# Query tiles and the last forget-head tiles as 512-column products in a two-layer fp32 trunk kernel

## The reference

```
h = h + 0.5 * swiglu(rms_norm(h, ffn1_norm), gate, up, down)       # 1024 -> 2816 -> 1024
h = h + token_mixing(rms_norm(h, mix_norm), w_in, ..., w_out)
h = h + 0.5 * swiglu(rms_norm(h, ffn2_norm), gate, up, down)
```

## Time and profile before

| what | us |
|---|---|
| median of 3 runs | 1005.8 (1005.06 to 1005.88) |
| the profiled execution | 1005.14 |
| its span, first to last instruction | 1003.3 |
| PE busy | 992.9 (99%) |
| PEld busy | 844.2 |
| DVE busy | 755.8 |
| ACT busy | 540.0 |
| POOL busy | 134.2 |

### The profile page before, as it was taken

The page is one execution under the profiler, slowest core; times in us unless marked ns, Lnnn a source line. Parts: engine busy times, 40 slices in busy tenths (PEclk is TensorE's granted clock), DMA queues, the critical chain, the costliest instruction groups (busy, mean ns, idle before and its releaser), DMA issues.

```text
span 1003.3 us, 16520 instructions
## 1 busy us (share of the span) xinstructions
PE 992.9 (99%) x5650; PEld 844.2 (84%) x5650; DVE 755.8 (75%) x1504; ACT 540.0 (54%) x978; POOL 134.2 (13%) x152
## 2 busy tenths in 40 slices
PE   9999999999999999999999999999999999999997
PEld 8888888888878888888888888889887788888885
DVE  6887777678667887777788777777786688777775
ACT  5555555566565555555555555555755555555553
POOL 1000000018761000000000000000197500000001
PEclk9999999999999999999999999999999999999999
DMA  8665555765534665555536555554563446555541
GB/s 297 205 205 188 187 187 188 251 225 173 208 106 151 218 196 188 188 188 188 189 128 212 191 187 189 187 187 148 185 210 131 167 150 223 191 188 188 188 146 42
DMA packets 38165, 184.76 MB, mean 184 GB/s; under 512 B 3904, under 2 KB 8176, under 8 KB 23920
## 3 DMA queue, kind: packets, MB, share of 16 engines
q1 hardware_dynamic: 33408, 178.60, 53.6%
q10 hardware_dynamic: 4720, 5.67, 1.8%
HBM read 183.18 MB, written 2.64 MB: 185 GB/s over the span
## 4 chain that ended last, share of the span: by engine, by line
PE 98%; DVE 1%; DMA 0%; ACT 0%; POOL 0%; issue 0%; DVEq 0%
PE ps L627 33%; PE ps L628 17%; PE ps L621 13%; PE ps L623 12%; PE ps L622 12%; PE ps L707 1%; PE ps L637 1%; PE ps L872 1%; PE ps L641 1%; PE ps L638 1%; PE ps L884 1%; PE ps L863 1%; PE ps L859 1%; DMA cst<-consts 0%; DVE wlo L1092 0%; PE ps L717 0%
## 5 line engine op out<-in xcount | busy, mean ns | idle before, releaser
L627 PE MATMUL ps<-xboth,whi 128*128 128x512 f32 x1440 | 508.0, 395 | 0.0
L628 PE MATMUL ps<-xboth,wlo 128*128 128x256 f32 x1440 | 403.4, 280 | 0.0
L627 PEld LDWEIGHTS ps<-xboth,whi 128*128 128x128 f32 x1440 | 269.9, 187 | 63.9 <-issue 1.0
L628 PEld LDWEIGHTS ps<-xboth,wlo 128*128 128x128 f32 x1440 | 272.0, 189 | 3.6
L1092 DVE TENSOR_TENSOR wlo<-raw,whi 128x1024 fp32r<-128x1024 f32 (+2 forms) x215 | 251.4, 1206 | 6.0 <-ACT whi L366 5.3
L366 ACT CAST whi<-raw 128x1024 fp32r<-128x1024 f32 (+1 forms) x222 | 217.5, 1029 | 7.4 <-PE ps L623 7.4
L1098 DVE TENSOR_TENSOR wlo<-raw,whi 128x1024 fp32r<-128x1024 f32 (+1 forms) x110 | 132.8, 1208 | 101.6 <-ACT whi L370 101.5
L408 ACT ACTIVATE sig<-hg 128x256 f32<-128x256 f32 x88 | 36.9, 420 | 199.0 <-DVE hg L1171 182.4
L370 ACT CAST whi<-raw 128x1024 fp32r<-128x1024 f32 (+1 forms) x112 | 112.8, 1007 | 53.4 <-PE ps L623 53.0
L623 PE MATMUL ps<-whi,hlo 128*128 128x512 f32 x352 | 138.9, 395 | 0.0
L622 PE MATMUL ps<-wlo,hhi 128*128 128x512 f32 x352 | 138.8, 394 | 0.0
(11 more groups left out here) (174 smaller groups left out, 1185.4 us busy)
## 6 DMA issues: line engine op xcount, KB each, us to landing
raw<-stream SPq DMA_DIRECT2D x111, 1024.0 KB, 5.2
raw<-stream SPq DMA_DIRECT2D x113, 512.0 KB, 3.6
decay<-table ACTq DMA_DIRECT2D x2, 1024.0 KB, 8.8
table<-table ACTq DMA_DIRECT2D x1, 1524.0 KB
X<-x SPq DMA_DIRECT2D x2, 512.0 KB, 5.4
bias<-table ACTq DMA_DIRECT2D x1, 1024.0 KB, 5.5
out<-feat SPq DMA_DIRECT2D x3, 256.0 KB, 2.4
cst<-consts SPq DMA_DIRECT2D x1, 576.0 KB, 11.2
```

Of the source, the lines that this page charges most:

```text
L627: nc.tensor.matmul(ps[:, bank, :], a[0], xboth[:, k, :], start=k == 0, stop=False)
L628: return nc.tensor.matmul(ps[:, bank, 0:S], a[1], xhi[:, k, :], start=False, stop=k == KT - 1)
```

## The change

All tiles of token mixing that were made by `three` are made by `wide`, in the same order on PE.

- The four index-query tiles: ACT's `query_out` copies the bank's second half to `tlo` instead of the whole result to `feat` (new semaphore `qlo_out`), at the same places of ACT's list. A new `query_sum` on DVE adds the first half and writes `feat`, and now it is what raises `qi_out`. Its four calls are put into DVE's list: after az, after logf (ahead of cn), and around the first half of `front(3)`.
- The last four forget tiles become `wide_tile(8)` to `wide_tile(11)` in the same two banks: ACT gets `tile_low(8)` to `tile_low(11)`, where it had only waited; DVE gets `tile_sum(8)` to `tile_sum(11)` in place of `tile_out`; POOL gets four more `scale`, between its `share` calls, and its two additions to `decay` come two heads later.

```diff
-NWIDE = 8
+NWIDE = 12
...
-                scale(l, 4, NWIDE)
+                scale(l, 4, 8)
                 for hh in range(2 * NH):
                     share(l, hh)
-                    if hh == 1:
+                    if hh in (0, 1, 3, 4):
+                        t = 8 + (0, 1, 3, 4).index(hh)
+                        scale(l, t, t + 1)
+                    if hh == 3:
                         pool.wait_ge(decay_in, (l + 1) * 16)
                         pool.wait_ge(const_in, 16)
-                    if hh in (1, 3):
+                    if hh in (3, 5):
...
                     act.wait_ge(feat_mm, l * NFEAT + j + 1)
-                    nc.scalar.copy(feat[:, j, :], ps[:, GU + j % 2, 0:S]).then_inc(qi_out, 1)
+                    nc.scalar.copy(tlo[j % 4], ps[:, GU + j % 2, S:2 * S]).then_inc(qlo_out, 1)
...
                     if p == 0:
-                        act.wait_ge(feat_mm, l * NFEAT + (FX + 5))
+                        tile_low(8)
                         front(7)
-                        act.wait_ge(feat_mm, l * NFEAT + (FX + 6))
+                        tile_low(9)
                         back(7)
                     if p == 1:
-                        act.wait_ge(feat_mm, l * NFEAT + NFEAT)
+                        tile_low(10)
+                        tile_low(11)
...
-                        t = three(ps[:, bank + j % 2, 0:S], w(s, at + k * P, P), xt(k), k == 0, k == KT - 1)
+                        t = wide(GU + j % 2, w(s, at + k * P, P), k)
...
-                    if g and h2 < 2:
+                    if g:
                         pe.wait_ge(scaled_out, l * NWIDE + (6 + 2 * h2))
-                    elif g:
-                        pe.wait_ge(feat_out, l * NTILE + (2 * h2 - 1))
...
-                tile(FX + 4, front(5), UNIT, bank=FILLB)
-                tile(FX + 5, back(5), FRONT, bank=FILLB)
+                wide_tile(8, front(5), UNIT)
+                wide_tile(9, back(5), FRONT)
...
+                def query_sum(j):
+
+                    dve.wait_ge(qlo_out, l * NQI + j)
+                    nc.vector.tensor_tensor(feat[:, j, :], ps[:, GU + j % 2, 0:S], tlo[j % 4], ALU.add).then_inc(qi_out, 1)
...
                                                op1=ALU.max).then_inc(az_out, 1)
+                query_sum(QI)
                 dve.wait_ge(css_mm, l + 1)
...
                 nc.vector.tensor_tensor(logf[:], mz[:], lz[:], ALU.subtract).then_inc(logf_out, 1)
+                query_sum(QI + 1)
                 dve.wait_ge(crows_mm, l + 1)
                 nc.vector.tensor_tensor(cn, ct, ps[:, CB, 0:S], ALU.mult).then_inc(cn_out, 1)
...
-                front(3)
+                query_sum(QI + 2)
+                front(3, (0,))
+                query_sum(QI + 3)
+                front(3, (1,))
...
                     if p == 0:
-                        tile_out(FX + 4, FILLB)
+                        tile_sum(8)
                         front(7)
-                        tile_out(FX + 5, FILLB)
+                        tile_sum(9)
                     if p == 1:
                         back(7)
-                        tile_out(FX + 6, FILLB)
                         turned(0)
-                        tile_out(FX + 7, FILLB)
+                        tile_sum(10)
                         turned(1)
+                        tile_sum(11)
```

More of the change, by code:

```diff
@@ L66 @@
 NQI = KA - QI
-NWIDE = 8
-NTILE = 1 + NFEAT - QA - NWIDE
+NWIDE = 12
 G_FFN1, G_MIX, G_FFN2, G_CKV, G_BF = 0, KT, 2 * KT, 3 * KT, 3 * KT + 1
@@ L183, in trunk, with tile_bank @@
         NPAIR = NH
-        TILEB = 5, 4, 3, 2
+        def tile_bank(t):
+            return (5, 4, 3, 2)[t % 4] if t < 8 else (3, 2)[t % 2]
         tlo = [t[:, i, :] for t in (ur, ht) for i in range(2)]
@@ L206, in trunk @@
         feat_mm, feat_out, ka_out, qi_out, wo_mm = sems("feat_mm feat_out ka_out qi_out wo_mm")
-        tlo_out, tsum_out, scaled_out = sems("tlo_out tsum_out scaled_out")
+        qlo_out, tlo_out, tsum_out, scaled_out = sems("qlo_out tlo_out tsum_out scaled_out")
         part_out, xg_out, fin_act = sems("part_out")[0], sems("xg_out0 xg_out1"), sems("fin_act")[0]
@@ L342, in _ @@
                 split_front(l, 5, 1)
-                scale(l, 4, NWIDE)
+                scale(l, 4, 8)
                 for hh in range(2 * NH):
                     share(l, hh)
-                    if hh == 1:
+                    if hh in (0, 1, 3, 4):
+                        t = 8 + (0, 1, 3, 4).index(hh)
+                        scale(l, t, t + 1)
+                    if hh == 3:
                         pool.wait_ge(decay_in, (l + 1) * 16)
                         pool.wait_ge(const_in, 16)
-                    if hh in (1, 3):
-                        nc.gpsimd.tensor_tensor(decay[:, :, (hh - 1) * P:hh * P], decay[:, :, hh // 2 * P + P:hh // 2 * P + S],
+                    if hh in (3, 5):
+                        at = (hh - 3) // 2
+                        nc.gpsimd.tensor_tensor(decay[:, :, 2 * at * P:(2 * at + 1) * P], decay[:, :, (at + 1) * P:(at + 2) * P],
                                                 cmask[:, P:S].unsqueeze(1).to_broadcast([P, NH, P]), ALU.add
@@ L512, in tile_low @@
                     act.wait_ge(feat_mm, l * NFEAT + (QA + t + 1))
-                    nc.scalar.copy(tlo[t % 4], ps[:, TILEB[t % 4], S:2 * S]).then_inc(tlo_out, 1)
+                    nc.scalar.copy(tlo[t % 4], ps[:, tile_bank(t), S:2 * S]).then_inc(tlo_out, 1)
                 relu_head(0)
@@ L566, in mix @@
                         act.wait_ge(vf_mm, l * 2 * 4 + 2 * 4)
+                        act.wait_ge(scaled_out, (l + 1) * NWIDE)
                         for b in range(NB):
@@ L796, in back, with tile @@
                     return m % 2
-                def tile(j, s, at, midway=None, bank=GU):
-                    if QI + 2 <= j < QA:
+                def tile(j, s, at, midway=None):
+                    if j >= QI + 2:
                         pe.wait_ge(qi_out, l * NQI + (j - 2))
[L804 to L807, removed]
                     for k in range(KT):
@@ L821, in wide_tile @@
                     else:
-                        pe.wait_ge(tsum_out, l * NWIDE + (t - 3))
+                        pe.wait_ge(tsum_out, l * NWIDE + (t - 3 if t < 8 else t - 1))
                     for k in range(KT):
-                        u = wide(TILEB[t % 4], w(s, at + k * P, P), k)
+                        u = wide(tile_bank(t), w(s, at + k * P, P), k)
                     u.then_inc(feat_mm, 1)
@@ L938, in index @@
                                          start=True, stop=True).then_inc(idx_mm, 1)
-                pe.wait_ge(feat_out, l * NTILE + 1)
+                pe.wait_ge(feat_out, l + 1)
                 pe.wait_ge(cn_out, l + 1)
@@ L983, in mix @@
                 logits(0)
-                tile(FX + 4, front(5), UNIT, bank=FILLB)
-                tile(FX + 5, back(5), FRONT, bank=FILLB)
+                wide_tile(8, front(5), UNIT)
+                wide_tile(9, back(5), FRONT)
                 logits(1)
-                tile(FX + 6, front(6, 0), 0, bank=FILLB)
+                wide_tile(10, front(6, 0), 0)
                 turn(0)
-                tile(FX + 7, front(6), UNIT, bank=FILLB)
+                wide_tile(11, front(6), UNIT)
                 turn(1)
@@ L1266, in tile_sum @@
                     dve.wait_ge(tlo_out, l * NWIDE + (t + 1))
-                    nc.vector.tensor_tensor(tsum[t % 4], ps[:, TILEB[t % 4], 0:S], tlo[t % 4], ALU.add
+                    nc.vector.tensor_tensor(tsum[t % 4], ps[:, tile_bank(t), 0:S], tlo[t % 4], ALU.add
                                             ).then_inc(tsum_out, 1)
```

## The result

The changed kernel is slower: median 1012.44 us (1009.31 to 1014.58, 4 executions) against 1005.84 (1005.06 to 1006.24), a ratio of 1.0066 with the 95% interval 1.0052 to 1.0079. The forecast was 1009.2 with a range up to 1012.4: the way was right, the size was not, and the median lies just outside the range.

What follows compares the result with a forecast made beforehand. PE was taken as the bound nearly everywhere, DVE's chain from cn before QI+3. DVE's wait +4.5 and shorter tiles -1.1 made +3.4 us, 1008.5 for the profiled execution, 1009.2 us for the median; range 1008.2 to 1012.4.

Steps and rivals of the forecast that it cites:

- The bound and the place: PE bounds nearly everywhere, but before QI+3 in each layer DVE's chain from cn does, with no slack behind cn.
- The costly step: QI+1's addition ahead of cn on DVE waits for ACT's copy behind three casts: 2.25 us a layer, +4.5 us.
- The tiles: QI+3 and four fill tiles behind PE's wait, each 0.11 us shorter as wide tiles: -1.1 us for both layers.
- QI's, QI+2's and QI+3's additions: DVE's other query additions, after az and around front(3): margins or idle time absorb them, cost nothing.
- the fill tiles: Last four forget tiles' new work on ACT, DVE and POOL: cost nothing, at most 0.3 us a layer.
- POOL's queue: Scalings added between POOL's shares: margins of 4.6 and 5.0 us before the transposes, cost nothing.
- One margin: Second head's transposes on PE after DVE's copy of the first head's: margin shrinks from 0.8 to 0.35 us.
- PE's clock falls in the longer stop: Rival, chance 0.27: PE's 2.9 us stop before QI+3 lowers its clock; 1010.8 us with one fall, 1012.4 with two.
- the likeliest case: The forecast itself, chance 0.60: longer waits before QI+3 but no clock fall, median 1009.2 us.
- The price of a fall: PE at the lower clock for as long as the 19 products at the start: 1.6 us each fall.
- The stop isn't there: Rival, chance 0.03: ACT copies QI+1 before its casts, so only the tiles' gain is left, 1004.1 us.
- The stalling fill stage: Rival, chance 0.07: PE waits at turn(1) or turn(2), 0.5 to 1 us a layer, 1010.2 to 1011.2 us.

Runs made afterwards that it cites:

- experiment 1: The changed kernel run again unaltered, against the kernel before: median 1013.11 us, ratio 1.0062.
- 2: The changed kernel with 22 products of 128x256 that nothing reads put into PE's stop in each layer: median 1009.47 us, ratio 1.0039.
- experiment 5: The kernel before with DVE waiting ahead of cn for ACT's copy of QI+1, then making two unread copies: median 1012.63 us, ratio 1.0076.
- experiment 3: The changed kernel with ACT's copy of QI+1 moved ahead of its casts of chunk 2: median 1004.50 us, ratio 0.9988.
- 7: The changed kernel with 22 unread products in only the first layer's stop (median 1011.04 us) or only the second's (median 1011.06 us).

## Why the prediction was wrong

**The bound and the place: right.** An off-path engine's order was the cost without the fall; cn's start (216.02 for 216.06) and QI+3's (218.75 for 218.81) came as worked out.

**The costly step, +4.5 us: right. The tiles, -1.1: a little too much.** The two executions of the changed kernel without a fall took 1009.31 and 1009.42, and 1009.47 was the median with the stop filled; the forecast was 1009.2. QI+3 came 2.19 us late in the first layer, where 2.25 was worked out. Of the tiles' gain the pace of 0.353 took some 0.6 us back in the profiled execution, so that the match of the sum is good to about half a microsecond and no better. The wait alone (2.37 us in place of 0.39, twice) gave +3.8 against 4.0 from its stop, and moving one line of ACT's list took it all away.

**QI's, QI+2's and QI+3's additions, the fill tiles, POOL's queue: cost nothing, right.** With the fill tiles alone the kernel is not slower, and with the copy ahead the whole change is faster than before. One margin was wrong. I had the second head's transposes wait with 0.35 us to spare for DVE's copy of the first head. In the changed kernel that copy ends at 262.93 + 0.54 = 263.47, and the transposes start at 265.10:

```profile
261.77 1.23 DVE L1099 TENSOR_TENSOR wlo<-raw,whi 128x1024 fp32r<-128x1024 f32 x1
262.93 0.54 DVE L1250 COPY prT<-ps 128x384 f32<-128x384 f32 x1
```

The split ahead of the copy takes 1.23 us where the same one took 2.13 in the kernel before:

```profile
259.32 2.13 DVE L1098 TENSOR_TENSOR wlo<-raw,whi 128x1024 fp32r<-128x1024 f32 x1
```

What lay beside it then was POOL's first addition to `decay`, 2.0 us long, and that has moved two heads on. I had moved this addition in POOL's queue but left DVE's durations as they were. That the overlap is what slowed the split was not tried by itself.

**The clock: the step that failed.** "PE's clock falls in the longer stop" stood among the rivals with 0.27, and the likeliest case was that the clock holds. By their mean clocks (0.992 to 0.995) it fell in 7 of the 9 executions of the changed kernel, and every one of the 7 is at 1012 or above. The rows for a better judgement were there: at the end of the span the clock had fallen after 2.7 us without work, and the new stop was reckoned at 2.9. Against this evidence I set only that "no two such stops need meet the same fate" and that this one stands between dense stretches. No row supported either, and the dense stretches on both sides did not keep the clock up. With the rows taken at their word the forecast would have been the one with a fall in each layer, 1012.4; the medians were 1012.44 and 1013.11. The Trainium skill (TensorE: Matmul & The Clock Gate, "The HAM clock gate") has idleness lower the clock and activity release it; experiments 1, 2 and 5 agree: the same wait with PE busy keeps a granted clock of 1.0, and the idle stops of 2.8 to 2.9 us lose it, down to 0.5, with the tiles of either kernel.

**The price of a fall: near in the middle, too narrow, and in part luck.** 1.6 us was worked out from the 19 products at the start, some 4.2 us at the lower level; the medians with one stop filled give 1.6 too. But no low stretch that was profiled was 4.2 us long: three were 3.4 us long and cost 1.3 to 1.5, two were 6.8 us long and cost 2.7. Two of the long ones make 5.4, which fits the changed kernel's highest execution, 1014.58; that both its falls were long is a reading of its time and its clock of 0.992, as it was not profiled. The range ended at the price of two middling falls, and had no room above it.

**The other rivals.** "The stop isn't there" did not happen, but its working, that all depends on whether the copy ends by 213.5, is what experiment 3 used: there the copy was ready when DVE came, and 1004.5 was measured where 1004.1 was worked out. The stalling fill stage did not happen.

What stays open: at which exact length of stop the clock falls, and why its moment and the length of the low stretch vary. Stops of 0.4 and 0.85 us left it alone, 2.1 and 2.4 brought at most small losses, 2.8 and 2.9 brought falls in most executions. All these stops stand behind four thin products that take 1.0 us (L922, 8 weight columns); whether these have a part in the fall was not tried.

## What to carry to other kernels

When an operation is cut in two over two engines (here a copy on ACT, an addition on DVE), the second half inherits the place of the first in the other engine's queue. Look up when that queue really gets to it, and what stands behind the new wait; here a wait of 2.9 us for a copy of 0.4 stood ahead of the one chain that PE waits for.

A stop of the matmul engine that comes near the length of one that already lowered the clock in the same trace should be priced with the fall, as the likely case and not as a rival. A spread of executions that follows the mean clock is its mark, and some useless matmuls in the stop (22 here) are a cheap test.

## What the runs showed of the hardware that was not expected

The fall need not come inside the stop. In the first layer of experiment 1 it came at 218.4, 0.8 us before PE resumed; in experiment 5 at 220.2, 1.3 us after PE had resumed and while it ran dense matmuls. Whoever looks only at the clock inside the idle stretch misses it.

The low level lasted 3.4 us in three of the falls profiled (experiment 1's second layer, 5 and 7) and 6.8 us in two (the first layer in experiment 1, and with only the second stop filled), though PE worked densely through nearly all of each.

At the lower level a pair of 512 and 256 columns took 0.64 us against 0.3465, 1.85 times and not twice as long.
